# Four cached rows in each of two stages: a new slot plan for the paged attention rows of a hybrid decoder step

## The chip, the cores and the metric

One core of one Trainium2 chip runs the whole program. The metric is the time that the device takes for one execution, in microseconds (us). Before the change it is 2083.97 us, the median of 3 runs (2073.3 to 2087.88).

## The reference, cut to what matters

One layer of a decoder step works on a prompt of 2048 tokens and on 8 sample rows of one token each. Both get a projection z = rmsnorm(x) @ w_in (1024 to 4096 columns), four heads of retention, four heads of differential attention, gates and an output projection. What the change moves is the attention of the 8 sample rows over their cached keys and values:

```python
past_k = cache_k[l][page_table].reshape(DEC_BATCH, past, H_DIFF, 2, DH_DIFF)   # 8 rows, 4096 positions, 512 numbers
past_v = cache_v[l][page_table].reshape(DEC_BATCH, past, H_DIFF, DV_DIFF)
...
s = jnp.einsum('bqhcd,bkhcd->bhcqk', q, k).astype(jnp.float32) * (DH_DIFF ** -0.5)
...
p = jax.nn.softmax(s, axis=-1)
a = p[:, :, 0] - lam * p[:, :, 1]
return jnp.einsum('bhqk,bkhe->bqhe', a, v.astype(jnp.float32))
```

A row has 32 pages of 128 positions. A page is 128 x 512 float32 numbers (256 KB) of keys and as much of values, so a row reads 16 MB and the eight rows 128 MB.

## The kernel before, in words

The program has four stages, one after the other, each a block in which the five engines run their own instruction lists and meet through semaphores; a block ends for all together.

**Stage 1** (`setup_stage`) normalises and turns x, and projects the sample rows. **Stage 4** (`final_stage`) is the output projection. The change touches neither.

**Stage 2** (`retention_stage`, from L765) has 64 tiles (4 heads x 16 chunks of 128 tokens). Its engines run `for s in range(RET_SLOTS)`, RET_SLOTS = 69. In slot s TensorE makes the projection of tile s as 8 chunks of three products (L1062 to L1064, high and low parts of the float32 operands), and between the chunks the small products of tile c = s - 2 (`turn`, `inner`, `outputs`). At the end of its slot it runs `row_values_pe` and `row_steps_pe`. VectorE has `row_keys_dve`, `next_state`, `row_steps_dve`, `rotate` and `gate_z` in one list per slot, GpSimd `rotate`, `row_keys_pool`, `scale_gates`, and in every fourth slot (s % 4 == 3) `finish` (L931 to L945). ScalarE makes the high parts. In the slots with s % 16 == 15 and 0 the weights of the next head are split (L866, L969).

**Stage 3** (`diff_stage`) has 64 tiles as well (4 heads x 16 query blocks) and SLOTS = 70 slots. In slot s TensorE makes the projection of tile s (L1598 to L1600) into a single PSUM bank, the scores of block a = s - 4, and the turned weights and values of block c = s - 5 (L1636, L1647). A block attends to all blocks before it, so the work of a slot grows with s % 16 and falls back at s % 16 = 4 or 5. GpSimd runs `norm_and_rope` in even slots, `row_keys_pool`, `scale_gates` in odd slots, `finish` in every fourth. In its slot 16k - 1 ScalarE splits the weights of head k: the first four chunks were loaded early, the last four are issued by SyncE at the very start of its slot 16k (L1222, called from `if 1 <= k < NH and t == 0`). ScalarE's list goes on from there with `keep_q`, `exponentials` and `keep_k`, whose kT the scores of the next slot read. The output weights are loaded from slot 56 on, and split in the slots 64 to 67, with loads that SyncE issues in the same list.

**The cached rows** ride along in stages 2 and 3. `class Rows` (L511 on) takes a first row, a ring depth and a plan, one entry per row: (slots of the keys, the last of these, slots of the values). A row's keys are 16 pairs of pages, spread evenly over the slots of the first list; its values are 8 groups of two pairs, spread evenly over the third list. The list `order` holds all pairs in the order of use, `due[s]` how many of them slot s has used by its end.

- `row_load` (L561) is SyncE's part: it keeps the ring `due[s] + depth - 1` pairs ahead. Pair n goes to ring buffer n % depth, and before its two page DMAs (L579) SyncE waits until pair n - depth has been used: a pair of keys when VectorE has reduced it, a pair of values when TensorE has finished its group. For the first pair of keys of a row it loads the row's query, too (L567), after a wait for all key products of the row before. SyncE works in order: all that stands behind such a wait in its list (tables, weights, stores) waits as well.
- `row_keys_pool` (L589): GpSimd multiplies a pair of keys, in place, by the query.
- `row_keys_dve` (L596): VectorE sums over 64 numbers to 16 scores per position. In stage 2 it does the pairs of slot s in slot s, in stage 3 in slot s + 1.
- `row_steps_dve`, `row_steps_pe`, `row_exp_act`: the softmax of a row, one small step per slot in the slots end + 1 to end + 5 (`end` is the plan's middle number); in slot end + 4 VectorE sums the weights (L622), and TensorE's product at the end of that slot waits for it (L647).
- `row_values_pe` (L671): for each group 4 pages, 8 matmul records of 128x512 (each float32 product shows as two). It waits for both pairs of a group, multiplies, and tells `values_used`.
- In slot own = last value slot + 1 VectorE picks each head's part (L628) and TensorE folds it (L650).

The ring has 7 buffers in stage 2 (`RET_ROWS = Rows(0, 7, ...)`) and 3 in stage 3 (`Rows(5, 3, ...)`). Groups of values per slot, before: in stage 2 a row has 8 groups in six slots (2, 1, 1, 2, 1, 1), the last row in four slots of two each. In stage 3 rows 5 and 6 have one group in each of eight slots, and row 7 has 2, 2, 1, 2, 1 in slots 64 to 68. Keys and values of stage 3 have no slot in common before the change.

A slot can be found in the trace: its first L1062 (stage 2) or L1598 (stage 3) product, 8 of which belong to each slot. By that stage 2's slot 0 begins at 121.0 us and its slot 63 at 704.0; stage 3's slot 0 begins at 740.7 and its slot 63 at 1695.8. The times of the slots named below were found so.

Of the kernel before, what the change touches and what calls it, by code (L numbers as in the profile page):

```python
# [698 lines left out]
SLOTS = TILES + OLAG + 1  # L699
# [27 lines left out]
def turn_order():  # L727
# [10 lines left out]
TURNS = turn_order()  # L738
TURN = {job: n for n, job in enumerate(TURNS)}

RET_PLAN = [
    (list(range(0, 9)), 8, [13, 14, 15, 16, 17, 18]),
    (list(range(11, 21)), 20, [25, 26, 27, 28, 29, 30]),
    (list(range(23, 33)), 32, [37, 38, 39, 40, 41, 42]),
    (list(range(35, 45)), 44, [49, 50, 51, 52, 53, 54]),
    (list(range(47, 57)), 56, [61, 62, 63, 64]),
]
DIFF_PLAN = [
    (list(range(3, 15)), 14, list(range(20, 28))),
    ([28, 29, 30, 32, 33, 34, 35, 36], 36, list(range(42, 50))),  # L750
    (list(range(50, 59)), 58, list(range(64, 69))),
]
DIFF_ROWS = Rows(5, 3, DIFF_PLAN, SLOTS)


RET_LAG = 2
# [4 lines left out]
TABLES = 4  # L761
RET_ROWS = Rows(0, 7, RET_PLAN, RET_SLOTS)

# [359 lines left out]
def diff_stage(nc, io, g):  # L1123
    R = DIFF_ROWS
    with ExitStack() as ctx:
# [1007 lines left out]
```

How the kernel before makes its waits and increments, by code:

```python
    def wait(self):  # L124
        self.eng.wait_ge(self.sem, self.base + self.n)
# [124 lines left out]
        @block.sync  # L250
# [1 line left out]
            def load_x(n):  # L252
                if n >= XB:
                    sp.wait_ge(h_ready, n - XB + 1)
                sp.dma_start(x_in[n % XB][0:rows[n], :], src[n]).then_inc(x_loaded[n % XB], 16)
# [1 line left out]
            def load_w(n):  # L257
                if n >= 2:
                    sp.wait_ge(z_ready, n - 1)
                sp.dma_start(w_raw[n % 2][:], w_groups[:, :, 512 * ORDER[n]:512 * ORDER[n] + 512]).then_inc(w_loaded[n % 2], 16)
# [24 lines left out]
            const(gqk_s[:, 0, :], io["q_norm_g"].to_broadcast([NS, DH]))  # L285
            const(gqk_s[:, 1, :], io["k_norm_g"].to_broadcast([NS, DH]))
            const(g.gout_ret[:], io["ret_out_g"].to_broadcast([P, P]))
            const(g.gout_diff[:], io["diff_out_g"].to_broadcast([P, P]))
            assert k == NCONST, k
            for n in range(1, 8):
                load_w(n)
                load_x(2 * n + 1)
                load_x(2 * n + 2)
            first = io["w_in"][0].rearrange("(c p) (m x) -> c p m x", p=P, x=P)
            sp.wait_ge(z_ready, 7)
            for c in range(DC):
                sp.dma_start(w_first[:, c, :].rearrange("p (m x) -> p m x", x=P), first[c, :, 0:4 * NH:NH, :]).then_inc(w_first_loaded, 16)
            sp.wait_ge(z_kept, 8)
            sp.wait_ge(rotated, 1)
            sp.dma_start(io["z_sample"], zs[:]).then_inc(stored, 16)
            sp.dma_start(io["new_k_sample"].rearrange("a b s h c d -> (a b s) (h c d)"),
```

## Time and profile before

| | us |
|---|---|
| runs: median (lowest to highest) | 2083.97 (2073.3 to 2087.88) |
| the profiled execution: its own time | 2075.96 |
| the profiled execution: span of the instructions | 2074.1 |
| stage 2, slots 0 to 62 | 583.0 |
| stage 2 from slot 63 to stage 3's first product | 36.7 |
| stage 3, slots 0 to 62 | 955.1 |
| stage 3 from slot 63 to stage 4's first load (1841.2) | 145.4 |
| stage 4 from there | 232.9 |

The rows below come from one profiled execution. A busy share says how long an engine had instructions running; a number in square brackets behind an instruction is how long its engine sat idle before it, and what ended that. PEclk is the share of TensorE's full clock (2.4 GHz) that was granted in a stretch; 0.5 is 1.2 GHz.

### The profile page before, as it was taken

To read this page: it belongs to the slowest core of one execution; us is meant where nothing else is said; L and a number is where in the kernel's file an instruction comes from. 1 tells how busy PE (TensorE), PEld (TensorE's weight loads), DVE (VectorE), ACT (ScalarE), POOL (GpSimd) and SP (SyncE) were. 2 spreads that over 40 slices of the span, in tenths; PEclk is the share of its full clock that TensorE was granted. 3 is DMA by queue.
4 is the path that set the end of the run, shared out by engine and by line. 5 is a ranking of instruction groups with operands and counts; after the bars stand their busy time and mean duration, and the time that the engine had idled before them with its cause. 6 is when DMAs were issued, how large, how long until landed. Compare 5 with 4: busy or idle time off the path is not lost. (4 is left out here: it accounts for less than half of the span.)

```text
span 2074.1 us, 28473 instructions
## 1 busy us (share of the span) xinstructions
PE 1675.0 (81%) x8308; PEld 1229.2 (59%) x8308; DVE 1097.0 (53%) x1947; ACT 721.5 (35%) x1947; POOL 1046.6 (50%) x1927
## 2 busy tenths in 40 slices
PE   6767788978988857888888888788886785569999
PEld 2256556655656545666756666666665663346786
DVE  2555565765676425666535777445576653314521
ACT  3222222321322223455544555444453454310010
POOL 4757685866666345764444568443557633210000
PEclk9989999988999977899999999999998997779999
DMA  7752656647547311311023122212212203334441
GB/s 282 267 163 71 199 190 192 221 133 219 170 163 228 119 41 47 101 47 61 6 97 123 46 77 72 62 51 80 89 52 87 82 21 107 101 101 141 133 137 67
DMA packets 169627, 240.99 MB, mean 116 GB/s; under 512 B 15393, under 2 KB 82090, under 8 KB 169458
## 3 DMA queue, kind: packets, MB, share of 16 engines
q1 hardware_dynamic: 164082, 222.33, 33.9%
q0 software_dynamic: 3072, 8.43, 1.1%
q10 hardware_dynamic: 2320, 8.42, 1.0%
q8 instruction: 68, 1.11, 0.2%
q14 instruction: 85, 0.70, 0.1%
HBM read 211.37 MB, written 27.76 MB: 115 GB/s over the span
## 5 line engine op out<-in xcount | busy, mean ns | idle before, releaser
L589 POOL TENSOR_TENSOR s_ring<-s_ring,s_q_row 128x1024 f32<-128x1024 f32 x128 | 316.4, 2486 | 111.6 <-DMA s_ring<-in_cache_k 108.3
L1598 PE MATMUL s_z<-g_w_hi,s_h_hi 128*128 128x512 f32 x512 | 240.6, 470 | 18.6 <-DVE s_h_lo L1493 14.3
L1062 PE MATMUL s_z<-g_w_hi,s_h_hi 128*128 128x512 f32 x512 | 231.0, 451 | 15.5 <-DVE s_h_lo L964 11.9
L1647 PE MATMUL s_o<-s_v,s_aT 128*128 128x128 f32 x1088 | 164.0, 291 | 72.9 <-ACT s_aT L1329 72.2
L1599 PE MATMUL s_z<-g_w_lo,s_h_hi 128*128 128x512 f32 x512 | 216.5, 423 | 0.0
L1600 PE MATMUL s_z<-g_w_hi,s_h_lo 128*128 128x512 f32 x512 | 215.6, 421 | 0.0
L1647 PEld LDWEIGHTS s_o<-s_v,s_aT 128*128 128x128 f32 x1088 | 136.6, 193 | 121.3 <-ACT s_aT L1329 120.0
L1064 PE MATMUL s_z<-g_w_hi,s_h_lo 128*128 128x512 f32 x512 | 208.3, 407 | 0.0
L1063 PE MATMUL s_z<-g_w_lo,s_h_hi 128*128 128x512 f32 x512 | 208.0, 406 | 0.0
L596 DVE TENSOR_REDUCE s_scores<-s_ring 128x16 f32<-128x1024 f32 x128 | 153.1, 1212 | 88.5 <-POOL s_ring L589 88.5
L1348 ACT ACTIVATE s_p<-s_sc,s_neg_max 128x1024 f32<-128x1024 f32 (+4 forms) x192 | 168.7, 888 | 12.3 <-DVE s_neg_max L1528 12.0
L1663 PE MATMUL s_sc<-s_kT,s_qT 128*128 128x512 f32 (+3 forms) x320 | 125.7, 393 | 32.2 <-ACT s_kT L1321 32.2
L1329 ACT COPY s_aT<-s_turn 128x512 f32<-128x512 f32 (+3 forms) x160 | 86.1, 538 | 185.3 <-PE s_turn L1636 185.3
L1598 PEld LDWEIGHTS s_z<-g_w_hi,s_h_hi 128*128 128x128 f32 x512 | 107.6, 210 | 54.7 <-issue 18.3
L964 DVE TENSOR_TENSOR s_h_lo<-g_hT,s_h_hi 128x512 fp32r<-128x512 f32 x128 | 131.5, 1029 | 14.6 <-ACT s_h_hi L861 4.2
L1062 PEld LDWEIGHTS s_z<-g_w_hi,s_h_hi 128*128 128x128 f32 x512 | 101.6, 198 | 59.2 <-issue 23.7
L1416 POOL TENSOR_TENSOR s_ssq<-s_ssq,g_pool_c 128x8 f32<-128x8 f32 x32 | 7.1, 223 | 240.8 <-DVE s_ssq L1505 240.8
L1269 ACT CAST s_h_hi<-g_hT 128x512 fp32r<-128x512 f32 x128 | 82.4, 644 | 128.2 <-PE s_z L1600 113.0
L1523 DVE TENSOR_REDUCE s_unit_min<-s_sc 128x1 f32<-128x1024 f32 (+7 forms) x128 | 120.9, 981 | 11.1 <-PE s_sc L1664 8.8
L1493 DVE TENSOR_TENSOR s_h_lo<-g_hT,s_h_hi 128x512 fp32r<-128x512 f32 x128 | 114.5, 895 | 17.9 <-ACT s_h_hi L1269 13.9
L1600 PEld LDWEIGHTS s_z<-g_w_hi,s_h_lo 128*128 128x128 f32 x512 | 106.1, 207 | 25.8
L1664 PE MATMUL s_sc<-s_kT,s_qT 128*128 128x512 f32 (+3 forms) x320 | 117.5, 377 | 0.0
(241 smaller groups left out, 3590.4 us busy)
## 6 DMA issues: line engine op xcount, KB each, us to landing
s_ring<-in_cache_k SPq DMA_DIRECT2D x256, 256.0 KB, 2.9
s_ring<-in_cache_v SPq DMA_DIRECT2D x256, 256.0 KB, 2.8
w_raw<-in_w_in SPq DMA_DIRECT2D x8, 2048.0 KB, 9.5
s_w_raw<-in_w_in SPq DMA_DIRECT2D x56, 256.0 KB, 4.6
x_in<-in_x_prompt SPq DMA_DIRECT2D x16, 512.0 KB, 5.3
s_table<-c_rope_ret SPq DMA_DIRECT2D x64, 128.0 KB, 3.1
u_scratch<-s_gate POOLq DMA_DIRECT2D x32, 256.0 KB, 2.7
s_u_in<-u_scratch SPq DMA_DIRECT2D x16, 512.0 KB, 4.9
```

Of the source, the lines that this page charges most:

```text
L589: pool.tensor_tensor(slot[:], slot[:], bc(R.q_row[:].unsqueeze(1), [P, 2, 512]), ALU.mult).then_inc(R.keys_times_q, 1)
L596: dve.tensor_reduce(R.scores[r % 2][:, 2 * j:2 * j + 2, :], R.slot(("k", r, j))[:].rearrange("p i (s f) -> p i s f", f=DH), AX, ALU.add).t ...
L964: dve.tensor_tensor(h_lo[n % 3][:], half_of_h(g, n % HALVES), h_hi[n % 3][:], ALU.subtract).then_inc(half_low, 1)
L1062: pe.matmul(b[:], hi[:, c, :], g.w_hi[:, wc, :], start=(wc == 0), stop=False)
L1063: pe.matmul(b[:], hi[:, c, :], g.w_lo[:, wc, :], start=False, stop=False)
L1064: last = pe.matmul(b[:], lo[:, c, :], g.w_hi[:, wc, :], start=False, stop=(wc == DC - 1))
L1348: act.activation(dst, score_bank[e % 2][:, 0:w], ACT.Exp, bias=neg_max[a % 2][:, m:m + 1], scale=-1.0, accum_out=sums[a % 2][:, m, u:u + 1 ...
L1598: pe.matmul(z_bank[:], hi[:, c, :], g.w_hi[:, wc, :], start=(wc == 0), stop=False)
L1599: pe.matmul(z_bank[:], hi[:, c, :], g.w_lo[:, wc, :], start=False, stop=False)
L1600: last = pe.matmul(z_bank[:], lo[:, c, :], g.w_hi[:, wc, :], start=False, stop=(wc == DC - 1))
L1647: last = pe.matmul(o_bank[:, 0:P], aT[:, x * P:(x + 1) * P], v[:, (c - i + kb) % VRING, :], start=(kb == 0), stop=(kb == i))
L1663: pe.matmul(b[:, at:at + w], qT[a % 2][:, m, :], keys, start=True, stop=False)
```

## The change

The eight rows are split four and four (before five and three), and both plans become regular. In stage 2 row r has its keys in slots 16r to 16r + 8, and its values in 16r + 14 to 16r + 17, so the first two key slots of a row are also the last two value slots of the row before. In stage 3 row r (the program's row 4 + r) has its keys in slots 17r to 17r + 7, two pairs in each, and its values in 17r + 13 to 17r + 16, two groups in each. The depths of the rings stay 7 and 3.

```diff
-RET_PLAN = [
-    (list(range(0, 9)), 8, [13, 14, 15, 16, 17, 18]),
-    (list(range(11, 21)), 20, [25, 26, 27, 28, 29, 30]),
-    (list(range(23, 33)), 32, [37, 38, 39, 40, 41, 42]),
-    (list(range(35, 45)), 44, [49, 50, 51, 52, 53, 54]),
-    (list(range(47, 57)), 56, [61, 62, 63, 64]),
-]
-DIFF_PLAN = [
-    (list(range(3, 15)), 14, list(range(20, 28))),
-    ([28, 29, 30, 32, 33, 34, 35, 36], 36, list(range(42, 50))),
-    (list(range(50, 59)), 58, list(range(64, 69))),
-]
-DIFF_ROWS = Rows(5, 3, DIFF_PLAN, SLOTS)
+RET_PLAN = [(list(range(16 * r, 16 * r + 9)), 16 * r + 8, list(range(16 * r + 14, 16 * r + 18))) for r in range(4)]
+DIFF_PLAN = [(list(range(17 * r, 17 * r + 8)), 17 * r + 7, list(range(17 * r + 13, 17 * r + 17))) for r in range(4)]
+DIFF_ROWS = Rows(4, 3, DIFF_PLAN, SLOTS)
```

## Rows read from the trace of the kernel before

**Rows 1.** The page: span, and busy time of each engine.

```profile
span 2074.1 us, 28473 instructions
PE 1675.0 (81%) x8308; PEld 1229.2 (59%) x8308; DVE 1097.0 (53%) x1947; ACT 721.5 (35%) x1947; POOL 1046.6 (50%) x1927
```

**Rows 2.** Windows by stage: stretch, length, busy time of engines, PEclk, DMA share, GB/s.

```profile
121.00:704.00 583.00, 496.55 (x2435) 367.43 (x2436) 352.35 (x704) 150.88 (x463) 386.89 (x482) 0.94 0.56 176
704.00:740.70 36.70, 17.11 (x92) 8.89 (x88) 11.62 (x27) 7.84 (x21) 14.40 (x41) 0.74 0.31 100
740.70:1695.80 955.10, 775.58 (x4090) 602.36 (x4090) 557.01 (x948) 451.11 (x1236) 536.75 (x1131) 0.93 0.21 67
1695.80:1841.20 145.40, 78.66 (x445) 55.53 (x444) 46.67 (x84) 51.75 (x118) 42.95 (x84) 0.78 0.25 78
```

**Rows 3.** Waits of the whole span: us in total, times, longest.

```profile
POOL s_ring L589 <- DMA s_ring<-in_cache_k: 108.3, 13, 18.7
...
PE s_row L647 <- DVE s_row_max L622: 29.4, 4, 7.6
PE s_row L671 <- DMA s_ring<-in_cache_v: 26.1, 11, 4.5
```

**Rows 4.** Groups of instructions on the cached rows, whole span.

```profile
L589 POOL TENSOR_TENSOR s_ring<-s_ring,s_q_row 128x1024 f32<-128x1024 f32 x128 | 316.4, 2486 | 111.6 <-DMA s_ring<-in_cache_k 108.3 <-POOL s_zqk L493 3.2
...
L596 DVE TENSOR_REDUCE s_scores<-s_ring 128x16 f32<-128x1024 f32 x128 | 153.1, 1212 | 88.5 <-POOL s_ring L589 88.5
...
L671 PE MATMUL s_row<-s_ring,s_scores 128*8 128x512 f32 x512 | 73.5, 662 | 26.1 <-DMA s_ring<-in_cache_v 26.1
```

**Rows 5.** Windows in stage 2: slots 0-9, 57-60, 61-62, 12, 55.

```profile
121.00:206.40 85.40, 70.82 (x319) 56.30 (x320) 48.06 (x97) 19.57 (x59) 61.58 (x55) 0.94 0.41 127
659.10:686.60 27.50, 27.50 (x143) 22.37 (x141) 16.95 (x45) 9.14 (x29) 14.39 (x31) 1.00 0.43 142
686.60:704.00 17.40, 17.40 (x102) 11.66 (x101) 7.58 (x24) 5.10 (x18) 3.56 (x6) 1.00 0.34 101
222.10:240.10 18.00, 7.22 (x38) 5.41 (x36) 9.02 (x17) 3.62 (x13) 14.99 (x24) 0.92 0.59 188
642.20:652.30 10.10, 7.82 (x40) 5.54 (x36) 6.92 (x17) 2.57 (x8) 8.63 (x16) 1.00 0.65 195
```

**Rows 6.** Timeline of TensorE, value groups of slot 64 and later two-group slots.

```profile
1727.82 1.04 PE L671 MATMUL s_row<-s_ring,s_scores 128*8 128x512 f32 x8
1732.40 1.90 PE L671 MATMUL s_row<-s_ring,s_scores 128*8 128x512 f32 x8 [3.53 <-DMA s_ring<-in_cache_v]
...
1804.14 1.89 PE L671 MATMUL s_row<-s_ring,s_scores 128*8 128x512 f32 x8 [3.61 <-DMA s_ring<-in_cache_v]
```

**Rows 7.** Windows in stage 3: slots 60-61, 3-14, 37-41, 53-57, 15-16, 31-32, 47-48.

```profile
1652.30:1680.80 28.50, 25.09 (x145) 20.21 (x144) 16.61 (x36) 15.50 (x44) 10.36 (x28) 1.00 0.10 29
764.70:934.60 169.90, 136.24 (x631) 108.23 (x631) 101.15 (x163) 70.72 (x207) 109.28 (x211) 0.85 0.19 61
1290.90:1353.70 62.80, 48.48 (x241) 38.55 (x239) 30.97 (x68) 26.84 (x85) 27.78 (x79) 0.92 0.17 51
1546.60:1620.40 73.80, 50.66 (x237) 40.33 (x234) 44.45 (x68) 26.56 (x85) 47.42 (x80) 0.86 0.22 67
934.60:972.50 37.90, 29.98 (x167) 23.16 (x165) 23.62 (x42) 22.24 (x55) 23.28 (x38) 0.95 0.20 62
1180.90:1221.60 40.70, 30.41 (x163) 23.80 (x162) 28.99 (x39) 22.01 (x54) 36.19 (x58) 0.92 0.27 81
1430.90:1476.70 45.80, 33.03 (x181) 24.56 (x177) 19.66 (x38) 22.07 (x55) 20.11 (x33) 0.89 0.25 76
```

**Rows 8.** Timeline at slots 47 and 48: SyncE, ScalarE, TensorE.

```profile
1434.65 16.42 SPq L579 DMA_DIRECT2D s_ring<-in_cache_v  x4
...
1455.04 0.62 ACT L1275 CAST g_w_hi<-s_w_raw 128x512 fp32r<-128x512 f32 x1 [8.02 <-DMA s_w_raw<-in_w_in]
...
1459.86 0.80 PE L1663 MATMUL s_sc<-s_kT,s_qT 128*128 128x512 f32 x1 [6.91 <-ACT s_kT L1321]
```

## The prediction, as it stood before the changed kernel was run

> **What bounds the kernel now.** I read the page first: TensorE is busy 81% of the span, the others about half or less [rows 1]. The windows by stage come next [rows 2]: in stages 2 and 3 TensorE is busy 85% and 81%, so there the time is TensorE's work plus the waits in its list, and the cached rows matter by what they add to that list. Then the waits [rows 3], and last the windows of single slots, which price a slot with and without cached work [rows 5, 7].
>
> Stage 2: four slots without cached work take 27.5 us, 6.9 each, with TensorE never idle; two slots with two value groups each and no keys take 17.4, 8.7 each [rows 5]. Over the 63 slots 583.0 - 63 x 6.9 = 148 us are due to five rows. A part of it is a collision: slot 12 is step end + 4 of row 0, and keys of row 1 are due in it, late behind GpSimd's `finish`. VectorE reduces them first, so L622 is late and TensorE waits: 18.0 us with 7.2 busy [rows 5]; four such waits, 29.4 us [rows 3], one for each row but the last.
>
> Stage 3: a slot without cached work in the heavy part takes 14.2 us at full clock (28.5 for two), TensorE idle 1.7 of it [rows 7]. In the tail, where a slot has two value groups, the second waits 3.5 to 3.6 us for its pages [rows 6]. That is the ring of 3: the first group holds two buffers, a pair of the second has the third, the other can be sent only when the first group is done. Rows 5 and 6, with one group per slot, show no such wait: stage 2's waits and three in the tail make up the eleven of L671 [rows 3].
>
> **The change, part by part.**
>
> *Stage 2, slots 0 to 62.* Row 0's keys stay: 85.4 us for slots 0 to 9 [rows 5]. Slots 10 to 13 become free of keys, four free slots cost 27.5 and 0.5 for the steps, whose operands are now early; slots 14 and 15 take 17.4. Sum 45.5. For a later row I take slots 16r to 16r + 9 like slots 0 to 9, since GpSimd sets their pace: 16 products of 2.49 us [rows 4] and two `finish` in 9 slots. To the 85.4 I add 3.8 for four value groups (8.7 - 6.9 = 1.8 for two, in slots 16r and 16r + 1) and 1.8 for L650's wait with keys in the same slot (slot 55: 10.1, 2.3 of it idle, partly there already [rows 5]): 91. Then four free slots 27.5 and two with values 18 at the border of heads: 136.5 per row, 273 for rows 1 and 2; 127.2 for row 3, without slot 63. In all 85.4 + 45.5 + 273 + 127.2 = 531, against 583: -52. From slot 63 on there are two groups in slot 65 more, a load chain of four pairs behind the ring: +4 (an estimate: four pairs, about 1 us each, in slots with little other work). Stage 2: -48. Bounds: the four collisions alone give -29, their idle time [rows 3]; with keys at the price of the best slots it is -62. I take -48, which rests on the windows of whole rows.
>
> *SyncE in stage 2.* Today it reaches the first keys of the next row while this row's are in work, and stands there with tables and weights behind it. After the change the values come first in `order`; tables and weights go out earlier. I count nothing: where this cost time it is in the windows that go. With keys and values in slots 16r and 16r + 1, six pairs are due per slot; the ring of 7 covers it but for about 1 us, and the other end is the wait of row 3's mean, 15.4 / 8 = 1.9 us (26.1 less the tail's 10.7).
>
> *Stage 3, value products.* Eight more groups of 1.04 us [rows 6]: +8.3. The same groups left stage 2 and are in its sum.
>
> *Stage 3, waits for values.* Now all four rows have two groups in each of four slots: 12 such slots among 13 to 50, each with 3.57 us of waiting (mean of the ends in rows 6), and one more in the tail: 13 x 3.57 = 46.4. Behind the wait stands TensorE's whole next slot. Bounds: 0 if TensorE had waited anyway for another engine, 4.5 each if the loads meet other traffic, the longest that the profile shows [rows 3]. I take the measured value: a heavy slot's 1.7 us of idle time lies between its own turns and copies, not at its end, and does not shrink when the slot starts late.
>
> *The clock.* In the tail the group behind the wait takes 1.90 us instead of 1.04 [rows 6]: half clock, 1.2 GHz. In slots 60 and 61 many short waits leave the clock at 1.00 [rows 7]. The new waits stand in slots of the second kind but have the length of the first. I take the row with the same wait: 0.86 on the group and about as much, 0.75, on the products behind it: 1.6 x 13 = 21. Bounds 0 and twice that. The Trainium skill, "TensorE: Matmul & The Clock Gate", section "HAM oscillation — how this bites in real kernels", says that a wait for a DMA in every tile lets the clock fall in every tile, so that the wait is paid twice; by it the sum stands, while by slots 60 and 61 alone it would be 21 less. The trace agrees with the rule in the tail and does not show it for a slot in the middle of a head.
>
> *The border of heads.* SyncE issues the last four weight chunks at the start of its next slot, and with values at the end of slots 15, 31 and 47 it stands in L579 until TensorE's last group. At slot 47 this can be seen: SyncE's loads take 16.4 us of its time, ScalarE waits 8.0 us for weights, TensorE 6.9 for kT [rows 8]. Slots 47 and 48 take 45.8 us; 15 and 16 (no values) 37.9; 31 and 32 (keys) 40.7 [rows 7]. Less the two groups, 2.1, that is 5.8 and 3.0 to be paid at two borders: +8.8. Bounds 0 and 16.
>
> *Stage 3, keys.* Row 4's keys now lie in slots 0 to 7, of which 0 to 2 have little other work; slots 3 to 14 take 169.9 us with 16 pairs now. Ten pairs in slots 3 to 7 and none behind: -2. Keys in slots 17 to 20 and 34 to 36 hide under heavy slots. In light slots they don't: slots 53 to 57 take 73.8 us with two pairs in most, slots 37 to 41 62.8 with none but a remainder [rows 7]. Two thirds of the 11 fall on slots 37 to 41, +8, and as slots 21 to 24 lose values at the same time, +3; slots 28 to 31 lose keys, -3. Sum +6, bounds -8 (the light slots cost nothing) and +25 (all nine light key slots at the 2.2 us of 53 to 57, 20, and 5 for the clock, 0.86 there).
>
> Stage 3: 8.3 + 46.4 + 21 + 8.8 + 6 = +90. Net 90 - 48 = +42. The profiled execution took 2075.96 us by its own time, so it would be 2118; the median of the runs lies 8.0 above it, so I predict 2084 + 42 = 2126.
>
> That "keys and values never in one slot" holds in stage 3 before as well; it brings nothing new there and I count nothing for it.
>
> **Rivals.**
>
> *A, faster: the waits for values are covered.* TensorE already waits in stage 3 for kT, aT and k_parts. If ScalarE and VectorE run behind TensorE there, 3.6 us at the end of a slot replace such waits. Then only products, keys and some rest remain: 8.3 + 6 + 13 x 0.3 = 18, net -30: 2054. For it speaks that TensorE is idle 19% of the stage [rows 2], against it that in the tail the next products ran on at once, slowly [rows 6]. It decides below 1.9 us per wait, clock and all: (48 - 8 - 6 - 9) / 13.
>
> *B, about the same.* The waits are there but the clock stays up and the borders cost nothing, since the wait gives ScalarE time: 90 - 21 - 9 = 60, and a part of the waits covered, 15: net -3 to +12, about 2090.
>
> *C, slower still: GpSimd becomes the bound of the light slots.* Two pairs in each of eight slots leave no slot to recover in; VectorE's reduction waits for the pair, and the turned q and k stand behind it. The wait of L589 for keys is already 108.3 us [rows 3]. Price: the upper bound of the keys, +19 on my sum, and half as much again, 10, for the clock: 2155.
>
> *D, stage 2 gains only the collisions.* -29 instead of -48: 2145. For it: GpSimd's pace in key slots is unchanged, and keys now meet values and the weight split in slots 16r.
>
> **How the numbers follow.** Forecast 0.50, A 0.08, B 0.17, C 0.13, D 0.12. A measurement of this kernel tells about 1% (21 us) from no change. Faster by over 1% is A: 0.08; within 1%, 2063 to 2105, is B: 0.17; slower the rest, 0.75. The range leaves out most of A and the far ends of C: 2085 to 2158. All of the likeliest case's own range, 2108 to 2145, is in it.
>
> **What would show it.** Right: L647's waits of 7.6 us gone and stage 2's slots 0 to 62 at 520 to 545 us; sixteen waits of L671 of about 3.6 us in stage 3, each followed by a group of 1.9; ScalarE waiting for weights and TensorE for kT at the starts of slots 16, 32 and 48; stage 3's slots 0 to 62 near 1040. Wrong: waits of L671 under 2 us, PEclk above 0.93 in stage 3, or a slot like 49 no longer than 18 us.

## The result and the profile after

Four runs of the kernel before gave a median of 2079.51 us (2073.30 to 2087.88), four of the changed kernel 2177.73 us (2172.31 to 2182.73). The ratio is 1.0469, its 95% interval 1.0416 to 1.0523: slower by 98 us, where +42 was forecast. The profiled executions have spans of 2074.1 and 2180.8 us, so they stand 106.7 apart; that of before was a quick one and that of after the slowest of its four, which makes up 8 us of the distance.

The page of the changed kernel, for [rows 1] and the keys' products in [rows 4]:

```profile
span 2180.8 us, 28473 instructions
PE 1727.0 (79%) x8308; PEld 1270.3 (58%) x8308; DVE 1097.4 (50%) x1947; ACT 722.2 (33%) x1947; POOL 1031.6 (47%) x1927
...
L589 POOL TENSOR_TENSOR s_ring<-s_ring,s_q_row 128x1024 f32<-128x1024 f32 x128 | 320.1, 2515 | 203.0 <-DMA s_ring<-in_cache_k 200.4
```

The instructions are the same in number; TensorE is busy 52 us longer with them. Windows by stage, for [rows 2] (stage 2's slots 0 to 62, its tail, stage 3's slots 0 to 62, its tail). The last one is counted here up to stage 4's first product, and in the kernel before it is 148.9 us long by that count:

```profile
123.50:669.90 546.40, 483.73 (x2349) 368.14 (x2349) 318.66 (x680) 150.87 (x462) 344.29 (x464) 0.95 0.49 153
669.90:703.70 33.80, 19.60 (x108) 9.70 (x104) 11.70 (x27) 7.84 (x21) 14.28 (x41) 0.82 0.53 161
703.70:1797.00 1093.30, 833.83 (x4161) 638.12 (x4161) 591.14 (x972) 452.12 (x1237) 565.22 (x1149) 0.87 0.24 74
1797.00:1952.20 155.20, 85.11 (x445) 60.70 (x443) 46.46 (x84) 51.65 (x118) 43.03 (x84) 0.72 0.24 78
```

Stage 2 gained 583.0 - 546.4 = 36.6 and 36.7 - 33.8 = 2.9, together 39.5. Stage 3 lost 1093.3 - 955.1 = 138.2 and 155.2 - 148.9 = 6.3, together 144.5. The net, 105, is all but 1.7 of the 106.7. In stage 3's slots 0 to 62 the busy time of TensorE rose by 58 and its idle time (length less busy) from 180 to 260. Three waits make up these 80 us: twelve for value pages, 45.0 in all (none before), those for `s_k_parts`, 126.1 us for 96.5, and those for kT at the starts of heads, 15.5 for 9.5. PEclk fell from 0.93 to 0.87. With only two levels, 1.2 and 2.4 GHz, 0.87 means that some 26% of the 1093 us stood at the lower.

The waits of the whole span, for [rows 3]:

```profile
POOL s_ring L589 <- DMA s_ring<-in_cache_k: 200.4, 29, 20.4
...
PE s_turn L1606 <- DVE s_k_parts L1503: 126.1, 33, 10.8
...
PE s_row L671 <- DMA s_ring<-in_cache_v: 61.4, 20, 4.6
...
PE s_o L1080 <- DVE s_inner_m L988: 51.0, 27, 4.5
...
PE s_sc L1653 <- ACT s_kT L1311: 38.5, 6, 10.4
```

L647's waits for VectorE (29.4 us before) are gone. Those for value pages rose from 26.1 to 61.4, GpSimd's for key pages from 108.3 to 200.4.

**Stage 2, slot by slot.** Windows of slots 0 to 9, 10 to 15, 16 alone and 16 to 25, for [rows 5]:

```profile
123.50:208.90 85.40, 72.40 (x319) 57.42 (x320) 50.38 (x97) 19.57 (x59) 61.06 (x55) 0.92 0.58 177
208.90:254.30 45.40, 45.40 (x242) 34.66 (x240) 23.47 (x63) 17.26 (x52) 20.02 (x49) 0.99 0.25 76
254.30:269.80 15.50, 11.01 (x55) 7.14 (x51) 13.97 (x22) 3.85 (x12) 8.93 (x6) 0.78 0.77 239
254.30:350.50 96.20, 80.47 (x376) 60.04 (x373) 59.48 (x114) 22.47 (x70) 69.58 (x77) 0.91 0.63 198
```

Slots without keys came out as priced (45.4 for slots 10 to 15 where 45.5 was forecast, and 44.9 for slots 26 to 31). A row's slots 16r to 16r + 9 take 96.2 where I had 91, and the excess shows in slot 16 (experiment 10 asks whether it is caused there): VectorE is busy 14.0 of its 15.5 us. Its timeline there, and the TensorE product that waited for it:

```profile
255.47 5.20 DVE L959 TENSOR_TENSOR g_w_lo<-s_w_raw,g_w_hi 128x512 fp32r<-128x512 f32 x4
...
263.34 0.28 DVE L988 TENSOR_TENSOR s_inner_m<-s_inner,s_mask 128x128 f32<-128x128 f32 x1
```

```profile
263.67 0.80 PE L1080 MATMUL s_o<-s_v,s_inner_m 128*128 128x128 f32 x2 [4.49 <-DVE s_inner_m L988]
```

The next head's weights are split in a run of four on VectorE just where the next row's keys begin. Slots 32 and 48 take 15.0 and 15.5 us in the same way.

**Stage 3 by stretches.** First the kernel before: slots 13 to 18, 30 to 35 and 47 to 51, which after the change hold the value groups; then slots 3 to 12, 21 to 29, 37 to 46 and 52 to 62. Slots 0 to 2, 19, 20 and 36 are left out; together they are 1.1 us shorter after the change.

```profile
905.40:1005.90 100.50, 85.83 (x490) 68.23 (x489) 68.12 (x119) 58.35 (x150) 58.03 (x126) 0.98 0.15 49
1165.90:1272.70 106.80, 89.53 (x508) 70.86 (x507) 82.82 (x120) 60.07 (x150) 82.28 (x136) 0.97 0.25 75
1430.90:1529.70 98.80, 80.93 (x462) 61.86 (x458) 58.52 (x94) 51.52 (x126) 43.83 (x81) 0.95 0.24 73
...
764.70:905.40 140.70, 110.47 (x486) 87.60 (x487) 78.49 (x124) 54.35 (x162) 90.78 (x167) 0.82 0.20 62
1041.50:1165.90 124.40, 103.21 (x553) 75.01 (x550) 59.32 (x119) 54.65 (x159) 55.95 (x142) 0.96 0.29 95
1290.90:1430.90 140.00, 116.09 (x614) 88.25 (x611) 71.47 (x144) 64.61 (x188) 66.58 (x187) 0.94 0.19 61
1529.70:1695.80 166.10, 126.58 (x656) 100.90 (x654) 100.61 (x169) 72.90 (x211) 108.72 (x226) 0.92 0.21 67
```

The same slots of the changed kernel:

```profile
877.90:1017.50 139.60, 106.92 (x551) 75.94 (x550) 63.08 (x114) 58.20 (x149) 51.14 (x106) 0.86 0.26 82
1189.80:1329.90 140.10, 108.04 (x574) 78.08 (x573) 66.38 (x114) 60.39 (x150) 55.86 (x115) 0.89 0.27 83
1499.20:1623.50 124.30, 93.45 (x501) 66.32 (x499) 53.59 (x95) 52.59 (x128) 46.16 (x101) 0.89 0.28 87
...
728.00:877.90 149.90, 106.17 (x492) 84.27 (x492) 86.20 (x132) 54.78 (x163) 90.21 (x181) 0.83 0.22 67
1053.00:1189.80 136.80, 104.94 (x500) 83.49 (x498) 79.05 (x132) 55.66 (x164) 73.09 (x162) 0.85 0.20 60
1346.80:1499.20 152.40, 119.32 (x573) 94.58 (x571) 88.47 (x151) 63.89 (x187) 92.03 (x197) 0.87 0.21 64
1623.50:1797.00 173.50, 133.08 (x655) 106.09 (x654) 107.23 (x170) 72.45 (x211) 102.36 (x208) 0.87 0.22 67
```

The three stretches with values went from 306.1 to 404.0 us, +97.9; the four others from 571.2 to 612.6, +41.4, although twelve value groups left slots 21 to 27 and 42 to 46 (a thirteenth left slot 20).

What a value slot holds: the second group in slots 13 and 33 (the wait is the same, what differs in slot 33 is told in the last section), and the first product of slot 48 that needs the new head's kT, for [rows 8]; then ScalarE's wait for the weight chunks there:

```profile
897.47 1.89 PE L671 MATMUL s_row<-s_ring,s_scores 128*8 128x512 f32 x8 [3.69 <-DMA s_ring<-in_cache_v]
...
1291.06 1.04 PE L671 MATMUL s_row<-s_ring,s_scores 128*8 128x512 f32 x8 [3.68 <-DMA s_ring<-in_cache_v]
...
1533.93 0.80 PE L1653 MATMUL s_sc<-s_kT,s_qT 128*128 128x512 f32 x1 [5.24 <-ACT s_kT L1311]
```

```profile
1529.12 2.13 ACT L1265 CAST g_w_hi<-s_w_raw 128x512 fp32r<-128x512 f32 x3 [13.63 <-DMA s_w_raw<-in_w_in]
```

And what a key slot holds, in slot 3 (17.8 us, 10.4 before, when the row's keys only began there): GpSimd, VectorE and TensorE, in the order of time.

```profile
725.31 2.37 POOL L589 TENSOR_TENSOR s_ring<-s_ring,s_q_row 128x1024 f32<-128x1024 f32 x1 [10.39 <-DMA s_ring<-in_cache_k]
```

```profile
739.86 1.22 DVE L596 TENSOR_REDUCE s_scores<-s_ring 128x16 f32<-128x1024 f32 x1 [3.97 <-POOL s_ring L589]
...
744.64 0.28 DVE L1503 TENSOR_TENSOR s_k_parts<-s_zqk,s_k_parts 128x128 fp32r<-128x128 f32 x1
```

```profile
744.97 0.75 PE L1606 MATMUL s_turn<-g_ident_r,s_q_parts 128*128 128x128 f32 x4 [10.82 <-DVE s_k_parts L1503]
```

GpSimd stands 10.4 us at a product whose pages aren't there, with the norm and turning of q and k queued behind it. VectorE then stands 4.0 us at a reduction (and 1.1 at the next), with `s_k_parts` queued behind them, and TensorE stands 10.8 us. This is the chain that my sum did not price. Twenty-four such waits for `s_k_parts`, of 2.8 to 10.8 us, stand in stage 3 in the key slots and in the slot behind each run of them.

### The profile page after: what moved, and what is told of

It reads as the page before. It is cut to its first block and busy times, and to the rows that moved or that the text cites. A ratio compares the mean times of both kernels' runs of the same rounds, so it can differ in the third digit from the quotient of the medians.

```text
span 2180.8 us, 28473 instructions
## 1 busy us (share of the span) xinstructions
PE 1727.0 (79%) x8308; PEld 1270.3 (58%) x8308; DVE 1097.4 (50%) x1947; ACT 722.2 (33%) x1947; POOL 1031.6 (47%) x1927
## 3 DMA queue, kind: packets, MB, share of 16 engines
q1 hardware_dynamic: 164082, 222.33, 32.7%
## 5 line engine op out<-in xcount | busy, mean ns | idle before, releaser
L589 POOL TENSOR_TENSOR s_ring<-s_ring,s_q_row 128x1024 f32<-128x1024 f32 x128 | 320.1, 2515 | 203.0 <-DMA s_ring<-in_cache_k 200.4
L1588 PE MATMUL s_z<-g_w_hi,s_h_hi 128*128 128x512 f32 x512 | 256.1, 500 | 13.4 <-DVE s_h_lo L1483 9.1
L1052 PE MATMUL s_z<-g_w_hi,s_h_hi 128*128 128x512 f32 x512 | 229.0, 447 | 12.2 <-DVE s_h_lo L954 12.2
L1589 PE MATMUL s_z<-g_w_lo,s_h_hi 128*128 128x512 f32 x512 | 231.2, 451 | 0.0
L1590 PE MATMUL s_z<-g_w_hi,s_h_lo 128*128 128x512 f32 x512 | 227.6, 444 | 0.0
L1054 PE MATMUL s_z<-g_w_hi,s_h_lo 128*128 128x512 f32 x512 | 208.5, 407 | 0.0
L1053 PE MATMUL s_z<-g_w_lo,s_h_hi 128*128 128x512 f32 x512 | 207.8, 406 | 0.0
L1653 PE MATMUL s_sc<-s_kT,s_qT 128*128 128x512 f32 (+3 forms) x320 | 129.3, 404 | 38.5 <-ACT s_kT L1311 38.5
L1588 PEld LDWEIGHTS s_z<-g_w_hi,s_h_hi 128*128 128x128 f32 x512 | 117.3, 229 | 54.7 <-issue 20.1
L1606 PE MATMUL s_turn<-g_ident_r,s_q_parts 128*128 128x128 f32 x256 | 39.5, 289 | 128.1 <-DVE s_k_parts L1503 126.1
L1590 PEld LDWEIGHTS s_z<-g_w_hi,s_h_lo 128*128 128x128 f32 x512 | 115.0, 225 | 29.0
L1483 DVE TENSOR_TENSOR s_h_lo<-g_hT,s_h_hi 128x512 fp32r<-128x512 f32 x128 | 121.3, 948 | 12.1 <-ACT s_h_hi L1259 8.0
L1052 PEld LDWEIGHTS s_z<-g_w_hi,s_h_hi 128*128 128x128 f32 x512 | 102.0, 199 | 42.5 <-DVE s_h_lo L954 12.5
L1589 PEld LDWEIGHTS s_z<-g_w_lo,s_h_hi 128*128 128x128 f32 x512 | 116.5, 228 | 16.7
L671 PE MATMUL s_row<-s_ring,s_scores 128*8 128x512 f32 x512 | 76.8, 693 | 61.4 <-DMA s_ring<-in_cache_v 61.4
```

The lines of the kernel that those rows point to most:

```text
L589: pool.tensor_tensor(slot[:], slot[:], bc(R.q_row[:].unsqueeze(1), [P, 2, 512]), ALU.mult).then_inc(R.keys_times_q, 1)
L1052: pe.matmul(b[:], hi[:, c, :], g.w_hi[:, wc, :], start=(wc == 0), stop=False)
L1053: pe.matmul(b[:], hi[:, c, :], g.w_lo[:, wc, :], start=False, stop=False)
L1054: last = pe.matmul(b[:], lo[:, c, :], g.w_hi[:, wc, :], start=False, stop=(wc == DC - 1))
L1588: pe.matmul(z_bank[:], hi[:, c, :], g.w_hi[:, wc, :], start=(wc == 0), stop=False)
L1589: pe.matmul(z_bank[:], hi[:, c, :], g.w_lo[:, wc, :], start=False, stop=False)
```

## The experiments

Three causes were to be told apart in stage 3: the waits for value pages (with the clock behind them), the keys (more of them, and closer together), and the borders of heads. Ratios are to the kernel before, on the same chip.

**1. The first value group of a slot taken out of the queue's end.** TensorE does it after the seventh of the eight weight chunks; the second stays where it was, so that the loads behind the first have the rest of the slot to land.

```
 def row_values_pe(pe, R, s, part=None):
-    for r, j in R.values.get(s, []):
+    for n, (r, j) in enumerate(R.values.get(s, [])):
+        if part is not None and (n == 0) != (part == 0):
+            continue
...
                     products(s, range(6, 7))
+                row_values_pe(pe, R, s, 0)
...
-                row_values_pe(pe, R, s)
+                row_values_pe(pe, R, s, 1)
```

> The changed kernel, but in stage 3 TensorE does the first value group of a slot after the seventh chunk of the projection and only the second at the slot's end, so that its buffers are free some 5 us before the second group needs its pages. Work and plan unchanged. Theory (the wait of the second group on a ring of 3, and the half clock that follows it, make most of stage 3's loss): the waits of L671 in stage 3, 59.7 us, fall to under 10, half-clock time in slots 13 to 16, 30 to 34 and 47 to 51 falls, and the whole comes to 2178 - 50 (waits) - 30 to 45 (clock) = 2083 to 2098. Rival (the fourth row's work and the denser keys make the loss, the wait covers other waits): the wait reappears at other places and the time stays above 2140. Rival (waits alone, clock unchanged): about 2125.

2086.34 us, ratio 1.0023 (1.0001 to 1.0045). Windows of slots 13 to 18 and of the tail:

```profile
876.50:992.00 115.50, 95.85 (x551) 70.70 (x551) 63.19 (x114) 58.27 (x149) 52.44 (x106) 0.95 0.32 98
```

```profile
1727.90:1856.20 128.30, 75.22 (x445) 53.77 (x444) 46.29 (x84) 51.07 (x118) 43.03 (x84) 0.82 0.30 96
```

Slots 13 to 18 fall from 139.6 to 115.5, 30 to 35 from 140.1 to 118.2, 47 to 51 from 124.3 to 106.1, together 64.2, and the tail 26.9: 91.1 us for sixteen waits that summed to 59.7, so 5.7 us each, of which 3.7 is the wait. The medians say the same, 2177.7 - 2086.3 = 91. So the waits were the loss's largest part, and they are a matter of the place in the slot. The edit does not show that nothing else was lost: it also shortens the kernel before, in its tail. A ring of four buffers, the other way to take these waits away, was not run.

**2. The same edit in the kernel before.**

> The kernel before, both plans unchanged, with the first value group of a slot in stage 3 moved to the middle of TensorE's slot. Only the tail has slots with two groups: its three waits, 10.7 us, go, and with them half-clock time: theory -15 to -25 (in split_groups the tail fell from 155 to 128 us), 2058 to 2068. Rival (the tail waits for the output weights anyway): within 5 us of 2083.

2058.08 us, 0.9880 (0.9844 to 0.9916). The tail, with three such waits, falls from 148.9 to 128.8. Its slots 0 to 62 take 957.8, as good as the same. Against this kernel the changed plans, equally mended, cost 1.4%, 30 us (±9, by the intervals of the two ratios): there is a second loss, beside the values.

**3. The clock behind the wait.** In the changed kernel four products that nobody reads stand between a slot's two value groups, in the 12 slots below 64.

```
+        if fill is not None and n == 1:
+            fill(s)
...
+                for _ in range(4):
+                    pe.matmul(z_bank[:], g.ident[:], g.hT[:, 0, 0:512], start=True, stop=True)
```

> The changed kernel, and in the twelve two-group slots of stage 3 below slot 64 TensorE makes four float32 products of 128x512 between the two value groups, whose result nobody reads; it only fills the 3.7 us in which it would wait for the second group's pages. Plan, ring and loads unchanged. Theory (the wait costs more through the clock than by itself): the time from the first to the second group stays near 3.7 us, the half-clock time in and behind these slots falls, and with it 25 to 40 us of the whole: 2138 to 2153. Rival (the products behind a wait are slow for another reason, or the clock falls for the short waits of these slots): 2170 to 2190.

2158.27 us, 1.0375 (1.0326 to 1.0424): 20 us less than the changed kernel, with more work, and less of a gain than the 25 to 40 expected. Slot 13's two groups and the windows of slots 13 and 14, which in the changed kernel take 21.4 and 23.7 us at PEclk 0.90 and 0.86:

```profile
886.72 1.05 PE L673 MATMUL s_row<-s_ring,s_scores 128*8 128x512 f32 x8
891.40 1.04 PE L673 MATMUL s_row<-s_ring,s_scores 128*8 128x512 f32 x8
```

```profile
872.50:892.40 19.90, 18.18 (x98) 11.76 (x96) 12.77 (x27) 10.84 (x31) 7.60 (x22) 1.00 0.14 41
892.40:913.70 21.30, 18.55 (x102) 12.08 (x98) 8.70 (x18) 8.51 (x23) 7.76 (x25) 1.00 0.40 124
```

The filling takes the place of the wait (the second group still begins 3.6 us after the first ends) and gives back only what the clock had cost: 20 / 12 = 1.7 us per wait. By the intervals of the two ratios the 20 are ±15, so this price is rough. The profiles give 19.3 for slots 0 to 62 (1093.3 less 1074.0). The second group runs in 1.04 instead of 1.89 us. The Trainium skill, "TensorE: Matmul & The Clock Gate", section "HAM oscillation — how this bites in real kernels", says that a wait for a DMA in every tile sends the clock down in every tile, so that slow products are paid on top of the wait. The trace agrees, in the middle of a head as well: from the start of each of the sixteen second groups PEclk is 0.50 to 0.72 over the next 6 us. The second payment, 1.7, is about half the first, 3.7.

**4. Stage 2's part alone.** The new stage 2 plan of four rows with the old stage 3. Row 4 is left out of the computation, and row 3's results are stored in its place.

> Stage 2's part alone: the new RET_PLAN of four rows with stage 3 exactly as before the change (rows 5 to 7, old plan). Row 4 is left out of the computation (the results of row 3 are stored in its place, by two more small stores). Theory: stage 2 gains what the changed kernel's trace shows, 36.6 us up to slot 62 and 2.9 behind it, and stage 3 is untouched: 2080 - 39 = 2041. Rival (stage 3 is slower in the changed kernel partly because stage 2 hands it something different, as a clock or a late start): stage 3's slots 0 to 62 differ from 955 us by more than 10.

2050.43 us, 0.9853 (0.9819 to 0.9886), -31. Its windows of stage 2, 545.1 and 35.2, give -39.4, as in the changed kernel. Stage 3, whose schedule is that of before, took 968.0 and 156.5 us with PEclk 0.92 and 0.70, for 955.1 and 148.9 with 0.93 and 0.77: 20 us more. But this profile is of the slowest of four executions (2058.31, 8 above their median) and that of before of a quick one, so it is no measure of the 8 us between -39 and -31. The kernel with stage 2's rows at a period of 12 (experiment 8), with the same schedule of stage 3 too, took 961.7. One profile of a stage is thus good to about 10 us. The 12.9 us in slots 0 to 62 are over the 10 that my rival had been given; it is neither shown nor ruled out, and it is small beside the 138 to be explained.

**5. Stage 3's plan with three rows.** Five rows in the old stage 2; the first three entries of the new stage 3 plan.

> Stage 2 as before (five rows, old plan), stage 3 with the changed plan's first three rows only (rows 5 to 7; slots 51 to 69 have no cached work). All eight rows are computed. Theory (the density costs, not the number of rows): slots 0 to 50 of stage 3 take what they take in the changed kernel, about 900 us against 771 before; slots 51 to 62 lose their keys (-18) and the tail its values (-25): +85, 2165. Rival (the fourth row costs, the plan does not): within 20 us of 2080.

2149.09 us, 1.0343 (1.0309 to 1.0377). Without a fourth row the new plan costs 3.4%, some 70 us. Slots 0 to 62 take 1062.3 us (+107), with all 12 two-group slots in them, and the tail 111.8 (-37), with none. The rival that the fourth row alone makes the loss falls. The fourth row is not free either: slots 0 to 62 take 31 us more with it (1093.3), 28 of them in slots 52 to 62, which take 173.5 with its keys and 145.8 without any cached work.

**6. Is it the keys?** In stage 3 only 64 of the 512 columns of the keys are multiplied and reduced; loads, order and waits stay. The rest of the scores is left out of the computation. Once with the changed kernel's plans, once with those of before, both with edit 1.

```
-        pool.tensor_tensor(slot[:], slot[:], bc(R.q_row[:].unsqueeze(1), [P, 2, 512]), ALU.mult
+        w = 512 if R.first == 0 else 64
+        pool.tensor_tensor(slot[:, :, 0:w], slot[:, :, 0:w], bc(R.q_row[:, 0:w].unsqueeze(1), [P, 2, w]), ALU.mult
```

> split_groups, with only 64 of 512 columns of each key page multiplied and reduced in stage 3 (the other scores are zero): the loads, the ring and all waits stay, GpSimd's and VectorE's work on keys falls to about an eighth. Theory P (the engines' work makes the keys' cost in stage 3): the key slots fall to the price of free slots, 40 to 60 us less, 2030 to 2045. Theory R (ring and loads): less than 15 us of gain. With both true in part: between.

> The kernel before with the first value group in the middle of the slot (before_split, 0.988 of before) and only 64 of 512 columns of each key page multiplied and reduced in stage 3, the other scores zero: the work on keys of three rows, in the old plan, taken away. small_keys against split_groups gave 78 us for four rows in the new plan, 19.6 a row. Theory N (the number of rows makes the missed cost): the same per row, 55 to 62 us less than before_split: about 1998. Theory D (the new plan's density makes it): clearly less per row, 25 to 40 us for the three: 2018 to 2033.

The changed plans: 2007.98 us, 0.9644 (0.9611 to 0.9677), 79 us less than with whole keys (1.0023), more than the 40 to 60 expected. Those of before: 2006.29 us, 0.9632 (0.9588 to 0.9675), 52 less (0.9880), between what my two theories had. Slots 0 to 62 of stage 3, with whole and with narrow keys, first by the changed plans:

```profile
701.90:1727.90 1026.00, 806.26 (x4162) 622.78 (x4162) 602.17 (x972) 452.15 (x1237) 571.27 (x1149) 0.90 0.25 79
```

```profile
703.90:1648.10 944.20, 783.09 (x4161) 605.21 (x4161) 474.93 (x972) 452.67 (x1237) 444.75 (x1149) 0.93 0.27 86
```

and by the plans of before:

```profile
744.10:1701.90 957.80, 782.67 (x4090) 609.13 (x4090) 560.65 (x948) 451.21 (x1236) 537.64 (x1131) 0.92 0.21 67
```

```profile
739.30:1648.00 908.70, 764.99 (x4090) 596.12 (x4090) 473.85 (x948) 451.11 (x1236) 441.62 (x1131) 0.95 0.22 70
```

The keys' arithmetic costs 81.8 us with four rows and 49.1 with three, 20.5 and 16.4 per row: the changed plans pay 33 us more for keys. Of these 16.4 are one more row at the old price, and 4 x 4.1 = 16.4 the higher price of each; by the medians, 79 against 52, it is 27 (±14, by the intervals of the four ratios), of them 17 for the row and 10 for the price. The row is clear of the noise, the higher price of each by itself is not.

Where the 81.8 lie is seen in TensorE's row: its idle time before L1606's turns, for `s_k_parts`, falls from 126.7 to 68.5 us, and its busy time with the same products by 23.2, as PEclk rises from 0.90 to 0.93. With three rows it is 96.4 to 64.9 and 17.7. The chain of slot 3 and the clock behind it are thus nearly all of the keys' cost.

By stretches, whole less narrow keys, the changed plans pay 19.0 us in slots 3 to 7, 11.4 in 21 to 29, 22.3 in 37 to 46 and 18.2 in 52 to 62. In slots 30 to 36, three of which have two pairs each, they pay nothing, and in slots 13 to 20 5.9 for eight pairs. The plans of before pay 14.1 in slots 3 to 12, 7.1 in 21 to 29, 6.8 in 30 to 36, 1.0 in 37 to 46 and 18.1 in 52 to 62. So heavy slots hide keys in good part (at most 6.8 us for ten pairs); it is the light ones that pay.

With narrow keys the two kernels take the same time, but not in the same places: by the windows stage 2 and its tail are 37 us shorter in the changed one, and stage 3's slots 0 to 62 36 us longer.

**7. What in the keys.** VectorE's reductions of the last slot's keys stand at the end of its slot, just before the work that ends in `s_k_parts`. Here they stand near its start, after the first split of h in the slot, so that a buffer comes free earlier. First with edit 1, then alone in the changed kernel.

```
                     split_h(2 * s + 1)
+                row_keys_dve(dve, R, s - 1)
...
-                row_keys_dve(dve, R, s - 1)
```

> split_groups, and in stage 3 VectorE reduces the pairs of slot s-1 at the start of its slot s instead of behind gate_z, so that ring buffers of keys come free about 7 us earlier in a slot. Theory R (the ring of 3 sets the key slots' pace: GpSimd's 178 us of waiting for key pages): GpSimd's wait falls by a third or more and slots 3 to 7, 21 to 25 and 37 to 41 lose 1 to 2 us each: -15 to -25. Theory P (GpSimd's own work of 2.5 us a pair and VectorE's 1.2 us in front of split_qk set it): no change beyond 8 us, or slower where VectorE then waits for GpSimd at the start of a slot.

> The changed kernel with the reductions of VectorE at the start of its slot in stage 3 (as in split_keysfirst) and the value groups left at the slot's end. Theory (keys' and values' costs add): -20 to -30, 2148 to 2158. Rival (they overlap; the slots of values set the time whatever the keys do): less than 10 us.

With edit 1: 2058.23 us, 0.9890 (0.9858 to 0.9922), 28 less than edit 1 alone. Alone: 2140.46 us, 1.0272 (1.0235 to 1.0309), 2.0% or some 40 less. Both are more than I had expected. The waits of the latter:

```profile
POOL s_ring L589 <- DMA s_ring<-in_cache_k: 132.0, 22, 19.7
...
PE s_turn L1606 <- DVE s_k_parts L1503: 101.9, 35, 10.0
```

Not one instruction is gone, and GpSimd waits 68 us less for key pages, TensorE 24 less for its turns. So a good part of what the keys cost is the place of the reductions. That it works through the ring of 3 (a buffer is free only when VectorE has reduced it, and a late reduction becomes a late load, a late product and a late `s_k_parts`) is my reading and not shown alone. The same edit takes the reductions, and VectorE's waits for them, from just before `s_k_parts`, and no run with a deeper ring tells the two apart. The sum of GpSimd's waits for pages is no price: with narrow keys it is higher (225.0 us for 170.8) in a kernel that is 79 us faster.

**8. The same on the kernel before, and a milder plan.** Edits 1 and 7 on the kernel before; and these with stage 2's rows at a period of 12 slots and an end for the collision of slot 12: keys in slots 12r to 12r + 7, values in 12r + 13 to 12r + 18. This plan was also run by itself.

> The kernel before, both plans unchanged, with both edits of stage 3: the first value group in the middle of the slot and VectorE's reductions at its start. before_split gave 0.988 of before. Theory (the ring of 3 holds GpSimd back here as well, 84.9 us of waits for key pages in stage 3 before): another -8 to -20, 2040 to 2052. Rival (with 1.3 to 2 pairs a slot the ring is enough): within 5 us of before_split, 2058.

> The kernel before with five rows in stage 2, but a period of 12 slots: keys in slots 12r to 12r+7, values from 12r+13, so that the softmax steps end+1 to end+4 fall into slots without keys. Stage 3 as before. Theory (the collision of L622 with the next row's keys costs about 8 us each, four times): the four waits of L647, 29.4 us, are gone, the denser keys cost part of that in waits for L998, as in the changed kernel (where they rose from 21 to 48 us for one row less): -5 to -20, 2060 to 2075. Rival (the collisions only move the idle time, GpSimd's total sets the pace): no difference beyond 5 us.

> before_both with stage 2's period of 12 slots (as in before_ret12, which gave 0.9973 of before). Theory: the gains add, 5 to 6 us less than before_both. Rival: nothing, because what stage 2 hands over changes stage 3's clock.

Edits 1 and 7: 2045.02 us, 0.9806 (0.9743 to 0.9868). By the medians that is 13 us below edit 1 alone, but the intervals overlap, and slots 0 to 62 of stage 3 take 955.9 for 957.8 although GpSimd's waits for key pages there fall from 89.5 to 37.5 us. In the looser plan the earlier reduction shows next to nothing in stage 3's slots. The period alone: 2077.31 us, 0.9973 (0.9953 to 0.9994): L647's waits go, but those of L671 for value pages rise from 26.1 [rows 3] to 47.4 us, so that of 29.4 us only 6 are won. All three: 2036.73 us, 0.9763 (0.9728 to 0.9798), the best kernel here that computes everything, 2.4% below before and, by the two ratios, 6.7% below the changed one. That the period still adds something on top of the two edits is not settled, for the intervals overlap.

**9. The borders.** To edit 1: the last four weight chunks are issued in the last slot of a head, ahead of the rows' loads.

```
-                if 1 <= k < NH and t == 0:
+                if k + 1 < NH and t == NT - 1:
                     for c in range(WRAW, DC):
-                        load_weights(k, c)
+                        load_weights(k + 1, c)
```

> split_groups, and the last four weight chunks of the next head are issued by SyncE at the head of its slot 15 of a head instead of slot 0 of the next, so they don't stand behind the row loads that wait for the last values. Theory (border of heads): TensorE's waits for kT at slots 16, 32 and 48, 19.4 us, fall to under 5, with some clock: 2086 - 15 to -25 = 2061 to 2071. Rival (ScalarE waits for GpSimd's weight split instead, since a chunk may be issued only when an earlier one is split): no gain beyond 5 us, the wait has another name.

2091.18 us, 1.0042 (1.0020 to 1.0063), no gain on 1.0023. The waits:

```profile
PE s_sc L1655 <- ACT s_kT L1313: 24.5, 4, 10.9
...
PE s_row L673 <- DMA s_ring<-in_cache_v: 25.7, 6, 8.0
```

With edit 1 alone they are 43.4 and 1.9. The waits for kT at the starts of slots 16, 32 and 48 are gone, but the weights are now issued ahead of the pages, and TensorE waits for pages instead: 50.2 us for 45.3 in all. The wait changed its place.

**10. Slot 16.** Edits 1 and 7, and stage 2's rows one slot later, so that keys don't begin in the slot of the weight split.

> split_keysfirst (0.989 of before, 2058) with all of stage 2's plan one slot later (keys 16r+1 to 16r+9, values 16r+15 to 16r+18), so that no keys lie in slot 16r, where VectorE splits the weights. Theory (the missing 15 us of stage 2 lie there: slots 16, 32 and 48 take 15 to 15.5 us with a wait of 4.5 for L988): slots 16, 32, 48 fall to about 10, -10 to -15 in stage 2, of which the later last values take 2 to 4 back: 2046 to 2054. Rival (the reductions only move: GpSimd, which runs through, is the bound): less than 4 us.

2068.79 us, 0.9917 (0.9885 to 0.9948), so not better than 0.9890. Windows of slots 16 and 18:

```profile
251.20:261.40 10.20, 8.99 (x54) 5.76 (x50) 8.06 (x17) 3.87 (x12) 5.03 (x8) 1.00 0.84 264
...
270.10:284.70 14.60, 9.60 (x53) 5.59 (x49) 7.80 (x18) 2.20 (x7) 8.47 (x7) 0.85 0.75 242
```

Against the changed kernel slot 16 lost 5.3 us as meant, but slot 18 gained 3.5, where TensorE now waits for value pages, and slots 16 to 25 take 97.8 for 96.2. Slots 0 to 62 of stage 2 stay at 545.9; its tail, where the last values now come a slot later, takes 42.9 for 34.1. My theory that the weight split costs stage 2 its missing 5 us per row falls; it only decides where they are paid. What sets the 96 us of a row's ten slots is left open.

## Why the prediction was wrong

The direction was right, the size was not: 2178 lies outside 2085 to 2158. Step by step:

- **Stage 2, -48.** It was -39.5. Slots 0 to 9, the free slots and the gone waits of L647 came as priced. The price of 91 for slots 16r to 16r + 9 was too low by 5 per row. The excess stands in the slots where VectorE splits weights, but experiment 10 moved it without removing it, so its cause is open. Slots 0 to 62 came to 546.4, just outside my own mark of 520 to 545. The tail gained 2.9 where I had +4, an estimate for which I had no row. (Two slips change nothing: four value groups at 1.8 for two are 3.6, not 3.8, and a slot 63 of 9 us leaves 127.5, not 127.2.) Off by 8.5 in all, half way to rival D.
- **Stage 3, value products, waits and clock, +8.3, +46.4 and +21.** The mechanism was right. There are sixteen waits, 59.7 us in all, so 3.7 each; ten are followed by a group of 1.89 or 1.90 us, three by one of 1.24 to 1.49, three by one of 1.04 to 1.06, so "each followed by a group of 1.9" was too strong, though half clock follows all of them. They cost 5.7 each with the clock by experiment 1, 1.7 for the clock alone by experiment 3, against 5.2 and 1.6 forecast. Taken as a difference, edit 1 gives back 94.2 us of stage 3 in the changed kernel and 17.4 in the one before, so 76.8 for thirteen more waits, where 46.4 + 21 = 67.4 was forecast: off by 9. Rival A, which wanted them under 1.9, is refuted, and B with it.
- **Borders, +8.8, and value products, +8.3.** All three borders now show a wait of 5.1 to 5.2 for kT, 15.5 us for 9.5 in two. With edit 1 in both kernels it is 19.4 for 5.3. What is left of stage 3's difference when edit 1 is in both (67.7 us) and the keys' share (32.7) is taken off is 35.0, where 8.8 + 8.3 = 17.1 was forecast: off by 18. The kT waits are 14 of the 35 and the eight groups net 8; the rest is not traced to one place, and the next point is a part of it.
- **Keys in stage 3, +6 (bounds -8 and +25): the step that failed.** By experiment 6 the keys' arithmetic costs 33 us more than in the kernel before by the windows, and 27 (±14) by the medians: clearly above +6, and at or beyond the upper bound. Heavy slots hide most of them, as I had assumed (0 us in slots 30 to 36, 5.9 in 13 to 20). What I had too low is the light slots. "Two thirds of the 11 fall on slots 37 to 41, +8": slots 37 to 46 pay 21 us more for keys than before. "Ten pairs in slots 3 to 7 and none behind: -2": slots 3 to 12 pay 6 more, through the chain of slot 3 above. I had priced those slots by how long slots with fewer keys were, and nowhere the wait of TensorE for `s_k_parts` behind a reduction that waits for its product, nor the half clock after it. Put per row, keys cost 15 to 18 us in the old plan and 17 to 22 in the new one, and there are four rows for three.
- **The groups that left light slots.** I counted eight groups net at full price, and so a full saving where they left. With narrow keys the four other stretches go from 537.7 to 534.6, -3 where twelve groups at 1.04 are 12.5. That TensorE had done them in time in which it now stands idle is not shown; the fourth row's narrow keys and loads are in the 534.6 too. Some 9 us.

By the windows the error is 105 - 42 = 63: keys 27, borders and groups 18, waits for values with the clock 9, stage 2 8.5. By the medians it is 98 - 42 = 56; the 7 between lie in which executions were profiled. Each of these terms rests on single profiles of a stage, so only the keys' and, less surely, the borders' stand clear of the 10 us of experiment 4. Rival C named the chain (VectorE's reduction waits for the pair, q and k stand behind it) and had 29 for it, against 27 by the windows and 21 by the medians. That GpSimd is the bound, as its title says, is not shown: in slot 3 it stood 10.4 us without pages. C with stage 2's miss would have been 2163, still 15 short.

## What to carry to other kernels

When work is moved between stages, price the work that arrives by itself, with and without it in the stage that takes it (here 15 to 22 us per row's keys), and by the kind of slot it lands in, before the moves inside the stage are priced. With this ring of three buffers, the place in a slot where a buffer is released was worth more than the plan of slots: two value groups apart gave 91 us, an earlier reduction 28 to 40 in the changed plan, and neither removed an instruction. A wait that is taken away at an in-order queue is gained only if nothing stands behind it: three edits (the borders, the shift, the period of 12) each removed the wait they aimed at and met it again at another.

## What the runs showed of the hardware

The half clock follows every one of the sixteen waits, but not always at once. In slot 13 TensorE waited 3.69 us and did the group behind in 1.89. In slots 30, 33 and 48 it waited 3.65 to 3.70 and did the group in 1.04 to 1.06, as at full clock, and the projection's products right after it were slow. In slot 33, where the group began at 1291.06, a product of 128x512 took 0.63 us, and a later one 0.39 again:

```profile
1292.55 0.63 PE L1589 MATMUL s_z<-g_w_lo,s_h_hi 128*128 128x512 f32 x1
...
1296.02 0.39 PE L1589 MATMUL s_z<-g_w_lo,s_h_hi 128*128 128x512 f32 x1
```

So the length of the one group behind a wait does not tell whether the wait took the clock; the products of the next microseconds have to be looked at as well. What sets the moment of the fall was not tried, and the price of 1.7 us is a mean.

The half clock spread further than the waits for pages. Behind the twenty-four waits of 2.8 to 10.8 us for `s_k_parts` in stage 3 PEclk is 0.50 to 0.74 over the next 6 us, and slots that hold neither keys nor values were slower than before the change: slots 60 and 61, 28.5 us at PEclk 1.00 [rows 7], now

```profile
1749.20:1781.90 32.70, 29.34 (x144) 23.54 (x144) 17.09 (x36) 15.50 (x43) 8.82 (x24) 0.84 0.14 42
```

with 4.2 us more busy time. The waits in these two slots are those of before, 1.64 us once in each, which there left the clock at 1.00. The first slow products stand behind a wait of 2.78 us in slot 59; a second stretch of them begins inside slot 60, and no longer wait stands before it. And the same stage with the same schedule took 955.1 and 968.0 us in two executions whose PEclk differed by 0.01: a difference of ten microseconds between stages of two profiles is not yet a finding.
